# A hybrid encoder layer on one core: the last four chunks of the residual turned on VectorE and through scratch memory

## What is computed

```python
h = x
f1 = swiglu_ffn(rms_norm(h, ffn1_pre_g), ffn1_w_in, ffn1_w_out)      # 2048 -> 2 x 5632 -> 2048
h = h + 0.5 * rms_norm(f1, ffn1_post_g)
mix = hybrid_mixer(rms_norm(h, mix_pre_g), w_in, ...)                # first a 2048 -> 8704 projection
h = h + rms_norm(mix, mix_post_g)
f2 = swiglu_ffn(rms_norm(h, ffn2_pre_g), ffn2_w_in, ffn2_w_out)
h = h + 0.5 * rms_norm(f2, ffn2_post_g)
```

## Time and profile before

| | |
|---|---|
| median of 3 runs | 2045.6 us (2045.48 to 2046.44) |
| the profiled execution: its own time | 2045.57 us |
| its span in the profile | 2043.8 us |
| granted TensorE clock, mean | 0.998 |
| TensorE matmuls busy | 2031.8 us, 99% |
| VectorE busy | 1226.4 us, 60% |
| ScalarE busy | 1052.4 us, 51% |
| DMA engines, data moved | 434.41 MB, mean 213 GB/s |

### The profile page before, as it was taken

The page is one execution under the profiler, slowest core; times in us unless marked ns, Lnnn a source line. Parts: engine busy times, 40 slices in busy tenths (PEclk is TensorE's granted clock), DMA queues, the critical chain, the costliest instruction groups (busy, mean ns, idle before and its releaser), DMA issues.

```text
span 2043.8 us, 26721 instructions
## 1 busy us (share of the span) xinstructions
PE 2031.8 (99%) x9016; PEld 1680.8 (82%) x9016; DVE 1226.4 (60%) x1942; ACT 1052.4 (51%) x1845; POOL 50.0 (2%) x86
## 2 busy tenths in 40 slices
PE   9999999999999999999999999999999999999998
PEld 7888888888888888888888888888888888888887
DVE  6655555655555576666666676755555656555554
ACT  7545544555444564545555555565555555544443
POOL 1000000000000011110000000000000000000000
PEclk9999999999999999999999999999999999999999
DMA  8787777777556659886666586577777777775554
GB/s 300 219 229 228 215 220 219 222 226 243 194 195 196 203 183 260 248 250 185 176 184 176 190 248 214 177 217 213 214 215 214 222 223 213 215 235 193 193 194 144
DMA packets 248908, 434.41 MB, mean 213 GB/s; under 512 B 16504, under 2 KB 49272, under 8 KB 248448
## 3 DMA queue, kind: packets, MB, share of 16 engines
q1 hardware_dynamic: 244496, 421.61, 68.0%
q0 software_dynamic: 4336, 11.82, 2.8%
HBM read 412.65 MB, written 20.70 MB: 212 GB/s over the span
## 4 chain that ended last, share of the span: by engine, by line
PE 99%; DVE 1%; DMA 0%; ACT 0%; issue 0%; SPq 0%; DVEq 0%; ACTq 0%
PE acc L1049 32%; PE acc L1051 32%; PE acc L1050 32%; PE tp L1162 1%; PE tp L1185 1%; PE tp L1173 0%; PE tp L1087 0%; DMA raw<-in_ffn_w_in 0%; DVE WL L683 0%; DVE h L778 0%; DVE smax L922 0%; DVE V L880 0%; ACT WH L441 0%; PE tp L1125 0%; DVE fg L751 0%
## 5 line engine op out<-in xcount | busy, mean ns | idle before, releaser
L683 DVE TENSOR_TENSOR WL<-raw,WH 128x512 fp32r<-128x512 f32 x1424 | 970.9, 690 | 776.4 <-ACT WH L441 774.8
L441 ACT ACTIVATE WH<-raw 128x512 fp32r<-128x512 f32 x1424 | 890.9, 631 | 938.0 <-PE acc L1051 873.8
L1049 PE MATMUL acc<-WH,XH 128*128 128x512 f32 x2032 | 799.1, 393 | 2.8 <-DVE WL L683 2.8
L1051 PE MATMUL acc<-WH,XL 128*128 128x512 f32 x2032 | 791.9, 390 | 0.0
L1050 PE MATMUL acc<-WL,XH 128*128 128x512 f32 x2032 | 791.4, 389 | 0.0
L1049 PEld LDWEIGHTS acc<-WH,XH 128*128 128x128 f32 x2032 | 381.9, 188 | 82.1 <-issue 4.1
L1051 PEld LDWEIGHTS acc<-WH,XL 128*128 128x128 f32 x2032 | 381.9, 188 | 80.0
L1050 PEld LDWEIGHTS acc<-WL,XH 128*128 128x128 f32 x2032 | 382.0, 188 | 78.0
L1049 PE MATMUL acc<-WH,MH 128*128 128x512 f32 x688 | 267.6, 389 | 0.0
L1050 PE MATMUL acc<-WL,MH 128*128 128x512 f32 x688 | 267.6, 389 | 0.0
L1051 PE MATMUL acc<-WH,ML 128*128 128x512 f32 x688 | 267.6, 389 | 0.0
(11 more groups left out here) (109 smaller groups left out, 667.7 us busy)
## 6 DMA issues: line engine op xcount, KB each, us to landing
raw<-in_ffn_w_in SPq DMA_DIRECT2D x352, 512.0 KB, 4.5
raw<-in_ffn_w_out SPq DMA_DIRECT2D x176, 512.0 KB, 4.6
raw<-in_w_in SPq DMA_DIRECT2D x136, 512.0 KB, 4.5
raw<-in_w_out SPq DMA_DIRECT2D x32, 512.0 KB, 4.7
turned_blocks<-Z SPq DMA_DIRECT2D x29, 512.0 KB, 3.1
Y<-turned_blocks SPq DMA_DIRECT2D x116, 128.0 KB, 4.7
raw<-in_w_up_a SPq DMA_DIRECT2D x16, 512.0 KB, 5.1
raw<-in_w_up_b SPq DMA_DIRECT2D x16, 512.0 KB, 4.4
```

What stands on the lines that cost most here:

```text
L441: act.activation(weight_hi(c), raw[:, c // 2 % RAW, c % 2, :], ACT.Copy).then_inc(hi_ready, 1)
L683: dve.tensor_tensor(weight_lo(c), raw[:, c // 2 % RAW, c % 2, :], weight_hi(c).bitcast(F32), ALU.subtract).then_inc(lo_ready, 1)
L1049: pe.matmul(a, hi[:, tok], weight_hi(c), start=first, stop=False)
L1051: return pe.matmul(a, lo[:, tok], weight_hi(c), start=False, stop=last)
```

## The change

The number of units that TensorE turns goes from 24 to 20 (`LATE = 4`). Feature chunks 12 to 15 (the last 512 features of `h`) are turned like the blocks above: `turn_late` on VectorE for each tile, once those features of `h` are updated, `Z` to `turned_blocks`, back into `Y`, then `late_hi` on ScalarE and `late_lo` on VectorE, chunk by chunk. TensorE's waits on the 24 units stay. The store stands ahead of the first load of the next sub-layer's second block, the fetch ahead of its third load. The counts of stored and fetched blocks behind them move by one.

```diff
+LATE = 4
-Z_QK = FFN_IN_BLOCKS // 2
+Z_N1 = FFN_IN_BLOCKS // 2
+Z_QK = Z_N1 + 1
 Z_MIX = Z_QK + 7
-Z_F2 = Z_MIX + OUT_BLOCKS - 1
+Z_N2 = Z_MIX + OUT_BLOCKS - 1
+Z_F2 = Z_N2 + 1
...
+        def by_tile(x):
+            return x.rearrange("p (t i s) -> p t i s", t=TT, i=4)
+
+        def late_turned(a):
+            return Y[:, :, :].rearrange("p t (i a s) -> p a t i s", i=4, a=4)[:, a, :, :, :]
...
-                load(c_in + begun, wi[(begun - DC) * P:, :], 2 * DC - begun, DFF)
+                load(c_in + begun, wi[(begun - DC) * P:, :], 2 * DC - begun, DFF, 0, z0 if z0 else None)
...
             for b in range(QK_BLOCKS + GATE_BLOCKS):
-                if 2 <= b < 2 + len(QK_HEADS):
+                if b == 1:
+                    load(C_QKV + b * DC, WIN, DC, b * NB, 0, Z_N1 + 1)
+                elif 2 <= b < 2 + len(QK_HEADS):
...
             def normed_hi(n, u):
-                act.wait_ge(xt_turned, UNITS * (n - 1) + u + 1)
+                act.wait_ge(xt_turned, (UNITS - LATE) * (n - 1) + u + 1)
...
+            def late_hi(n, a):
+
+                c = DC - LATE + a
+                act.wait_ge(blocks_landed, 64 * ((Z_N1 if n == 1 else Z_N2) + 1))
+                act.activation(by_tile(XH[:, c, :]), late_turned(a), ACT.Copy,
                                scale=gainT[:, n * DC + c:n * DC + c + 1]).then_inc(xt_hi, 1)
...
                 for j in range(OUT_BLOCKS):
                     for t in range(TT):
                         h_square(n, j, t)
-                    normed_hi(n, 20 + j)
+                    if j == 1:
+                        late_hi(n, 0)
+                    if j:
+                        late_hi(n, j)
...
+            def turn_late(n, t):
+
+                dve.wait_ge(h_ready, OUT_BLOCKS * (TT * (n - 1) + t + 1))
+                dve.transpose(Z[:, t, :].rearrange("p (j a s) -> p a j s", j=4, a=4),
+                              h[:, t, D - NB:D].rearrange("p (a j s) -> p a j s", a=4, j=4)).then_inc(blocks_turned, 1)
+
+            def late_lo(n, a):
+
+                c = DC - LATE + a
+                dve.wait_ge(xt_hi, DC + UNITS * (n - 1) + UNITS - LATE + a + 1)
+                dve.scalar_tensor_tensor(out=by_tile(XL[:, c, :]), in0=late_turned(a),
+                                         scalar=gainT[:, n * DC + c:n * DC + c + 1], in1=by_tile(XH[:, c, :].bitcast(F32)),
                                          op0=ALU.mult, op1=ALU.subtract).then_inc(xt_lo, 1)
...
                 for u in range(4, 6):
                     normed_lo(n, u)
+                turn_late(n, 0)
                 scaled(b_last, n - 1, 1)
                 for j in range(OUT_BLOCKS):
                     update_h(n - 1, 1, j)
                     for u in range(2 * j + 6, 2 * j + 8):
                         if j < 3:
                             normed_lo(n, u)
+                turn_late(n, 1)
                 split_lo(chunk + 9)
...
-                for u in range(20, UNITS):
-                    normed_lo(n, u)
+                for a in range(LATE):
+                    late_lo(n, a)
...
-                    if c % 2 and SKEW + c + 4 < UNITS:
+                    if c % 2 and SKEW + c + 4 < UNITS - LATE:
                         turn_h(n, SKEW + c + 3)
                         turn_h(n, SKEW + c + 4)
```

More of the change, by code:

```diff
@@ L342, in _ @@
                 load(C_UP + u * 16 + 8, UPB, 8, u * NB)
-            load(C_WOUT, WOUT, DC, 0, 0, Z_F2, 0, 0, Zmix, Ymix)
+            load(C_WOUT, WOUT, DC, 0, 0, Z_N2, 0, 0, Zmix, Ymix)
             for b in range(1, OUT_BLOCKS):
@@ L450, in normed_hi @@
                 c = unit_tile(u)[0]
-                act.wait_ge(xt_turned, UNITS * (n - 1) + u + 1)
+                act.wait_ge(xt_turned, (UNITS - LATE) * (n - 1) + u + 1)
                 act.activation(unit_of(XH, u), turned(u), ACT.Copy,
+                               scale=gainT[:, n * DC + c:n * DC + c + 1]).then_inc(xt_hi, 1)
+            def late_hi(n, a):
+                c = DC - LATE + a
+                act.wait_ge(blocks_landed, 64 * ((Z_N1 if n == 1 else Z_N2) + 1))
+                act.activation(by_tile(XH[:, c, :]), late_turned(a), ACT.Copy,
                                scale=gainT[:, n * DC + c:n * DC + c + 1]).then_inc(xt_hi, 1)
@@ L660, in _ @@
                     if b == 0 and c == 5:
-                        fetched_hi(Ymix, Z_F2 - 1, XH, 8)
+                        fetched_hi(Ymix, Z_N2 - 1, XH, 8)
                     if b == 0 and c == 14:
@@ L697, in normed_lo @@
                                          scalar=gainT[:, n * DC + c:n * DC + c + 1], in1=unit_of(XH, u).bitcast(F32),
+                                         op0=ALU.mult, op1=ALU.subtract).then_inc(xt_lo, 1)
+            def turn_late(n, t):
[7 more added lines that the diff above has]
+                                         scalar=gainT[:, n * DC + c:n * DC + c + 1], in1=by_tile(XH[:, c, :].bitcast(F32)),
                                          op0=ALU.mult, op1=ALU.subtract).then_inc(xt_lo, 1)
```

## The result

| | before | with the change |
|---|---|---|
| median | 2045.64 us (17 runs, up to 2046.82) | 2048.12 us (17 runs, 2046.74 to 2052.36) |
| ratio to before | | 1.0014, 95% interval 1.0008 to 1.0021 |
| the profiled execution | 2045.57 us, span 2043.8 | 2048.71 us, span 2046.9 |

The kernel is 2.5 us slower, 0.12 to 0.14%: inside 0.2%, but measurably on the slow side, and its executions spread over 5.6 us where those of before spread over 1.4.

A forecast was written before the change was run, and what follows sets the result against it. TensorE, its matmuls busy 99% of the span, was taken as the bound. Per change of phase -0.88 + 0.29 + 0.86, twice +0.54 us on 2045.57, gave 2046.1 us, range 2044.2 to 2048.6.

The forecast's parts named there:

- The likeliest case: TensorE waits at chunk 12 for the fetch, which lands from 746.3 to 749.0; likeliest 2046.1 us, chance 0.70.
- Transposes at 0.11 us each: On TensorE, 16 transposes go, priced from neighbouring matmuls' starts: -0.88 us per change of phase.
- The turn of tile 0 at nothing, the turn of tile 1 at 0.29: VectorE's added turns: the first hidden in its waits, the second delaying TensorE at unit 12 by 0.29 us.
- Arrival at chunk 12: TensorE would reach chunk 12 at 747.42, 0.59 us earlier than before.
- Store 3.1 us, first fetch at 740.75, last issue at 742.1: New path on SyncE: store landing in 3.1 us, then four fetch issues taking 1.81 us.
- The last fetch in 5.1 us: Last of four fetches needs 5.1 us to land, at 747.2; TensorE then waits 0.86 us at chunk 12.
- L: Time when all late fetches have landed, put at 747.2; TensorE starts chunk 12 1.08 us later.
- Transfers at nothing, in a stretch where the DMA engines are mostly idle: At each change of phase, 1 MB more of transfers was to cost nothing.
- Everything behind chunk 12 at nothing: Late units, next block's parts, loads and norm's root shift within their cover, at no cost.
- The fetch in time: Rival: landing by 746.3, so TensorE never waits at chunk 12; 2044.4 us, chance 0.19.
- Slower by over 0.2%: Rival: the fetch is the new bound, landing from 749.0 on; 2052.7 us at the longest fetch, 8.4 us; chance 0.09.

The follow-up runs named there:

- e5: Changed kernel without the late blocks' store and fetch and without VectorE's two turns (stale data, wrong results): 2043.58 us, ratio 0.9989.
- e1: Changed kernel without the late blocks' store and fetch, VectorE's two turns kept (stale data, wrong results): 2044.23 us, ratio 0.9993.
- e7: Changed kernel with late fetch one weight load earlier, and VectorE making units 12 and 13 before chunk 9's low part: 2044.09 us, ratio 0.9993.
- e9: As e7, with VectorE also making units 16 and 17 before chunk 13's low part: 2043.72 us, ratio 0.9991.
- e3: Changed kernel with the late fetch one weight load earlier in SyncE's queue: 2044.30 us, ratio 0.9994.
- e6: Changed kernel with the late fetch one weight load later in SyncE's queue, 5 executions: 2056.74 us, ratio 1.0052.
- e8: Changed kernel with the late fetch one weight load earlier, and SyncE waiting for its landing before the loads behind, one execution: 2044.24 us.
- e2: Changed kernel with SyncE waiting for the late fetch to land before issuing the weight loads behind it: 2047.01 us, ratio 1.0007.

## Why the prediction was right, and where it was off

The forecast was 2046.1 us, within 0.2%, with a range to 2048.6; 2048.1 lies in it, near its end, and 7 of the 17 executions lie above it. So the range held by a small margin, and with some luck: one term was over a microsecond short at each change of phase. The likeliest case, that TensorE waits at chunk 12 for the fetch, came in. Point by point, per change of phase unless said otherwise:

- *Transposes at 0.11 us each*: 0.88 predicted, 0.98 measured (e5). The sign of the choice was right: the starts, not the durations. The Trainium skill's 275 ns ("TensorE: Matmul & The Clock Gate", Part 4), which it gives for bf16, fits the duration recorded here in fp32, 272 ns, and not the cost in this busy queue.
- *The turn of tile 0 at nothing, the turn of tile 1 at 0.29*: 0.28 measured (e1 against e5). The first gap was where it was placed (738.23 for 738.27). The prediction saw that unit 16 would just fit behind the delay, but not what follows: the delay had two places to show, unit 12 and unit 16, so that to cure one alone wins little (e7), and both everything (e9).
- *Arrival at chunk 12*: 747.42 predicted, 747.47 measured.
- *Store 3.1 us, first fetch at 740.75, last issue at 742.1*: 3.19, 740.59 and 742.09.
- *The last fetch in 5.1 us*: this step failed: 6.26 and 6.5. L was 748.35, not 747.2, and chunk 12 started 1.17 us from 748.28, over the half microsecond that the prediction itself had set as the sign of a mispriced landing. Of the 2.6 us that the forecast change (0.54) misses of the one between the profiled executions (3.14), 2.5 are in this term: the wait at chunk 12 was 1.98 and 2.25, not 0.86. (By the medians 1.9 us are missing.) I took the nearest rows by their place in the program. The prediction named the circumstance, a second load just ahead of the fetch, and gave it half a microsecond; e3 against the changed kernel shows 3.2 us for it, and the table above what it hangs on. It is not the distance between the two issues alone: at the places of 4.6, 5.2 and 6.8 us the second load was issued 1.5, 2.4 and 1.2 us before the first fetch, but it landed 1.9, 2.2 and 4.4 us after the last fetch was issued, and the fetch 2.7, 3.0 and 2.3 us after that.
- *Transfers at nothing, in a stretch where the DMA engines are mostly idle*: this premise was wrong and belongs to the same failure. The windows of the kernel before (us, busy us of PE, PEld, VectorE, ScalarE and POOL, granted clock, mean busy share of the DMA engines, GB/s), and under them those of the changed one:

```profile
740.00:744.00 4.00, 4.00 (x21) 3.30 (x20) 3.55 (x8) 3.02 (x8) 0.00 (x0) 1.00 0.79 245
744.00:748.00 4.00, 4.00 (x23) 3.31 (x22) 1.25 (x3) 3.38 (x12) 0.00 (x0) 1.00 0.57 171
...
740.00:744.00 4.00, 4.00 (x22) 3.35 (x21) 3.66 (x9) 2.87 (x8) 0.00 (x0) 1.00 0.98 299
744.00:748.00 4.00, 3.62 (x16) 2.65 (x15) 0.56 (x1) 1.78 (x6) 0.00 (x0) 1.00 1.13 238
```

  The DMA engines were 0.79 and 0.57 busy already, and with the fetch and the loads around it the share is about 1 (packets overlap in the record, so it can pass 1).
- *Everything behind chunk 12 at nothing*: right, 5.57 against 5.58 us.
- *The fetch in time*: this rival was the right picture of e3, where one load fewer is ahead. The fit for one DMA that the prediction took from the Trainium skill ("DMA: Bandwidth & Descriptors", Anatomy of one DMA), 2.3 us for 128 KB, is given there for transfers that GpSimd issues, and these are issued by SyncE. It is under every landing of 128 KB on this path; the shortest is 2.5 us (one of the earlier three fetches of e8), the shortest of a last fetch 2.8.
- *Slower by over 0.2%*: as its mechanism says, it comes when the fetch is later still (e6, 2056.7 us). Its price was too low, as it left out the clock. Some executions of the changed kernel reached 2050 to 2052 us. A late landing, with or without a fall of the clock, would explain them, but they were not profiled, so that stays argued.

## What to carry to other kernels

When an operation is taken off the bounding engine and sent round through memory, the gain is the difference of the neighbours' starts, and the risk is the landing of the last transfer; put its issue ahead of every bulk load that isn't needed sooner, for its place in the queue was here worth three times the gain. When a transfer's time is read from another place in the trace, look at when the load just ahead of it lands there, and at the DMA share of the stretch, not only at what stands in the queue. A new instruction in a full engine queue delays everything behind it, so ask for each consumer what its slack is before one is cured.

## What was not expected of the hardware

- A wait of 2.85 or 4.59 us on TensorE was followed by about seven matmuls at 0.43 us a step, granted clock 0.55 and 0.61 in those stretches; waits of 1.83 and 2.10 us were not (clock 1.00).
- The last of four fetches of 128 KB landed 1.7 to 3.1 us after the 512 KB load just ahead of it in the queue, in the seven kernels of the table and at the three places of the earlier trace rows, while its time from issue went from 2.8 to 7.8 us.
- Loads that are issued behind a fetch in the same queue still make it later: by 1.1 us where a second load stands 0.4 us ahead (e2 against the change), by 0.2 to 0.5 us where none does (e8 against e3).
- Matmuls behind a group of transposes keep a step of about 0.23 us for a chunk or two in place of 0.227: with the starts of two groups at 0.88 us, this is the likely source of the other 0.10 us of the 0.98 that e5 shows per change of phase.
